# Parking x in eight pieces instead of one transfer, reloading it tile by tile, and loading p earlier, in one layer of a streaming encoder

## The reference

```
h = rmsnorm(x, g_mix_pre)
q_a, k_a, v_a, q_r, k_r, v_r, g_r, gate_a, gate_r = split_in(h @ w_in)
o_a = sliding-window attention with sinks (8 heads, 2 kv heads of 64)
o_r = retention (4 heads, key 128, value 256), group norm, * silu(g_r)
merged = sigmoid(gate_a) * (o_a @ w_branch_attn) + sigmoid(gate_r) * (o_r @ w_branch_ret)
x = x + rmsnorm(merged @ w_out, g_mix_post)
f = (silu(h @ w_ffn_gate) * (h @ w_ffn_up)) @ w_ffn_down      with h = rmsnorm(x, g_ffn_pre)
x = x + rmsnorm(f, g_ffn_post)
x = x + (p @ w_ple_proj) * sigmoid(x @ w_ple_gate)
```

## Time and profile before

| what | value |
|---|---|
| median of 3 runs | 1077.85 us (1077.6 to 1079.03) |
| span of the profiled execution | 1075.0 us (its own run time is not given) |
| TensorE, matmul busy | 1029.6 us, 96% |
| VectorE busy | 514.0 us, 48% |
| ScalarE busy | 333.8 us, 31% |
| GpSimd busy | 155.0 us, 14% |
| mean granted TensorE clock | 0.980 |
| DMA over the span | 88.63 MB, mean 82 GB/s |

### The profile page before, as it was taken

The page is one execution under the profiler, slowest core; times in us unless marked ns, Lnnn a source line. Parts: engine busy times, 40 slices in busy tenths (PEclk is TensorE's granted clock), DMA queues, the critical chain, the costliest instruction groups (busy, mean ns, idle before and its releaser), DMA issues.

```text
span 1075.0 us, 19829 instructions
## 1 busy us (share of the span) xinstructions
PE 1029.6 (96%) x7428; PEld 995.3 (93%) x7428; DVE 514.0 (48%) x855; ACT 333.8 (31%) x490; POOL 155.0 (14%) x162
## 2 busy tenths in 40 slices
PE   7999999999999999899949999999999999999697
PEld 5999899898999999899949999999999999999597
DVE  5554667666566433342295433432334444323842
ACT  5233434334434222123333322221222222222232
POOL 0221212121100000101272111100011111112500
PEclk9999999999999999999978999999999999999699
DMA  6722221221222232432211232223332322223032
GB/s 170 233 87 79 65 64 51 62 68 42 71 60 79 70 88 78 147 96 88 81 40 41 82 93 78 73 66 87 92 93 78 92 83 66 81 81 105 20 101 66
DMA packets 163818, 88.63 MB, mean 82 GB/s; under 512 B 14225, under 2 KB 162097, under 8 KB 163649
## 3 DMA queue, kind: packets, MB, share of 16 engines
q1 hardware_dynamic: 160256, 79.19, 25.6%
q0 software_dynamic: 1632, 7.23, 1.9%
q10 hardware_dynamic: 1888, 1.64, 0.5%
HBM read 82.08 MB, written 6.03 MB: 82 GB/s over the span
## 4 chain that ended last, share of the span: by engine, by line
PE 85%; DVE 5%; issue 3%; DMA 3%; ACT 1%; POOL 1%; POOLq 0%; DVEq 0%; SPq 0%; ACTq 0%
PE acc L467 77%; PE small L618 2%; DMA raw<-in_w_in 1%; PE small L633 1%; DMA raw<-in_w_branch_ret 1%; DVE wlo L1101 1%; DVE res L1417 1%; PE small L661 1%; PE small L665 1%; PE small L663 1%; ACT whi L790 1%; DVE yl L1428 1%; PE small L570 0%; ACT prob L850 0%; PE small L673 0%
## 5 line engine op out<-in xcount | busy, mean ns | idle before, releaser
L1101 DVE TENSOR_TENSOR wlo<-raw,whi 128x1024 fp32r<-128x1024 f32 (+3 forms) x156 | 181.1, 1161 | 337.4 <-ACT whi L790 337.0
L790 ACT ACTIVATE whi<-raw 128x1024 fp32r<-128x1024 f32 (+3 forms) x156 | 153.2, 982 | 436.9 <-PE acc L467 421.0
L467 PE MATMUL acc<-yh,whi 128*128 128x288 f32 x960 | 209.7, 299 | 25.3 <-DVE yl L1428 13.6
L467 PE MATMUL acc<-yh,wlo 128*128 128x288 f32 x960 | 208.2, 298 | 0.0
L467 PEld LDWEIGHTS acc<-yh,whi 128*128 128x128 f32 x960 | 156.2, 191 | 28.1 <-DVE yl L1428 14.9
L467 PE MATMUL acc<-yl,whi 128*128 128x288 f32 x832 | 179.5, 298 | 0.0
L467 PE MATMUL acc<-xh,whi 128*128 128x288 f32 x736 | 163.2, 303 | 2.1 <-DVE wlo L1101 2.0
L467 PE MATMUL acc<-xl,whi 128*128 128x288 f32 x736 | 157.4, 295 | 0.0
L467 PE MATMUL acc<-xh,wlo 128*128 128x288 f32 x736 | 156.8, 294 | 0.0
L467 PEld LDWEIGHTS acc<-yh,wlo 128*128 128x128 f32 x960 | 155.8, 191 | 0.0
L467 PEld LDWEIGHTS acc<-yl,whi 128*128 128x128 f32 x832 | 136.0, 192 | 0.0
(11 more groups left out here) (219 smaller groups left out, 1144.4 us busy)
## 6 DMA issues: line engine op xcount, KB each, us to landing
raw<-in_w_in SPq DMA_DIRECT2D x92, 256.0 KB, 3.1
raw<-in_w_ffn_gate SPq DMA_DIRECT2D x44, 256.0 KB, 3.1
raw<-in_w_ffn_up SPq DMA_DIRECT2D x44, 256.0 KB, 3.2
raw<-in_w_ffn_down SPq DMA_DIRECT2D x48, 192.0 KB, 2.4
raw<-in_w_branch_ret SPq DMA_DIRECT2D x16, 256.0 KB, 3.0
raw<-in_w_out SPq DMA_DIRECT2D x16, 256.0 KB, 2.9
raw<-in_w_ple_gate SPq DMA_DIRECT2D x16, 256.0 KB, 3.0
x_scratch<-x_t POOLq DMA_DIRECT2D x1, 2304.0 KB, 14.7
```

The lines of the kernel that those rows point to most:

```text
L467: ins = nc.tensor.matmul(acc[:, a, hf, 0:HALF], w[:, s, at:at + P], x(k)[:, hf * HALF:(hf + 1) * HALF], start=first and n == 0 and m == 0, ...
L790: nc.scalar.activation(whi[:, s, 0:n], raw[:, s, 0:n], ACT.Copy).then_inc(hi_ready, 1)
L1101: nc.vector.tensor_tensor(wlo[:, s, 0:n], raw[:, s, 0:n], whi[:, s, 0:n].bitcast(F32), ALU.subtract).then_inc(lo_ready, 1)
```

## The change

Four things change, nearly all in the stream of POOL:

- p and the caches are issued before `power(0)`, behind a new wait for the last quarter of x; the tables follow `power(0)`.
- x is parked by eight DMAs of one tile (288 KB) in place of one of 2304 KB. Two stand ahead of the first head, the others behind `head_job` of its six steps. They run in the first head alone (`isinstance(h, int)` is true only for the head that is written out).
- The reload of tile k waits for unit U_MRG2 + k instead of all eight for U_MRG2.
- Whoever waits for the park (ScalarE's first gate, POOL's reload) waits for all eight pieces.

```diff
@@ -937,7 +937,7 @@
                 if t == 0:
-                    act.wait_ge(x_saved, 16)
+                    act.wait_ge(x_saved, 16 * KD)
                 gate(w, a, sig[:, t // 2, t % 2, :])
@@ -1559,15 +1559,21 @@
             pool.dma_start(sink_row[:, :], sinks_in).then_inc(gains_in, 16)
-            power(0)
+            pool.wait_ge(x_in[QUARTERS - 1], 32)
             pool.dma_start(p_row[:, 0:RT - 1, :], p_p[0, 0].rearrange("(r p) n -> p r n", p=P)).then_inc(p_in, 16)
             pool.dma_start(p_row[0:DEC, RT - 1, :], p_s[0, 0]).then_inc(p_in, 16)
             pool.dma_start(ck_row[:, :], cache_k[0, 0].rearrange("n h d -> n (h d)")).then_inc(cache_in, 16)
             pool.dma_start(cva[:, :], cache_v[0, 0].rearrange("n h d -> n (h d)")).then_inc(cache_in, 16)
+            power(0)
             pool.dma_start(tab[:, T_ID + P:T_COLS], table_in[:, T_ID + P:T_COLS]).then_inc(tables_in, 16)
             pool.dma_start(rot[:, :, :], table_in[:, T_ROT:T_ALL].rearrange("p (a n) -> p a n", a=2)).then_inc(tables_in, 16)
-            pool.wait_ge(xt_copied, KD)
-            pool.dma_start(scratch, x_t[:, :, :].rearrange("p k n -> p (k n)")).then_inc(x_saved, 16)
+
+            def save_x(k):
+
+                if k == 0:
+                    pool.wait_ge(xt_copied, KD)
+                pool.dma_start(scratch[:, k * ROWS:(k + 1) * ROWS], x_t[:, k, :]).then_inc(x_saved, 16)
+
@@ -1632,6 +1638,8 @@
                     head_job(t, h, slot)
+                    if isinstance(h, int):
+                        save_x(t + 2)
                     pieces(2 * t + 1, r, rslot)
@@ -1644,15 +1652,17 @@
             pool.wait_ge(tables_in, 32)
+            save_x(0)
+            save_x(1)
             head(0, None, 0, None)
...
-            pool.wait_ge(unit_done, U_MRG2)
-            pool.wait_ge(x_saved, 16)
+            pool.wait_ge(x_saved, 16 * KD)
             for k in range(KD):
+                pool.wait_ge(unit_done, U_MRG2 + k)
                 pool.dma_start(res[:, k, :], scratch[:, k * ROWS:(k + 1) * ROWS]).then_inc(x_back, 16)
```

## The result

| | before | after |
|---|---|---|
| median of 4 runs | 1077.72 us (1077.05 to 1079.03) | 1070.98 us (1070.5 to 1071.94) |
| span of the profiled execution | 1075.0 us | 1068.7 us |
| mean granted clock | 0.980 | 0.983 |

The ratio is 0.9936 with a 95% interval of 0.9924 to 0.9948: the change takes 6.7 us (5.6 to 8.2) off. The direction was right, the gain was put too small by a quarter. Six more runs of the changed kernel later gave 1070.23 us, so the forecast missed by more than those 0.02 us. Where it comes from is mostly where the forecast looked for it, so the question is which terms were mis-sized.

What follows compares the result with a forecast made beforehand. TensorE, busy nearly throughout, was taken to bound the kernel, so time lay only in its stops and clock falls. Terms -0.53 and -4.50 took the span from 1075.0 to 1070.0; plus 2.85 gave 1072.8 us, range 1071.0 to 1075.3.

Steps and rivals of the forecast that it cites:

- Part 1: Start, POOL: p and caches ahead of power(0) wait for x and fall into an empty DMA stretch; cost 0.
- Part 4: First head: eight park issues on POOL, 0.55 us each, hide in its idle time; cost 0.
- the rival by the rule of the Trainium skill: First head: POOL's issues take some 3 us there, rotation comes 2.3 us late; 1075.1 us, chance 4%.
- Part 5: First head: each parked tile adds 1.0 us to a weight load (0.95 from one load), within spare time; cost 0.
- Part 6: Second merge: reloading x one tile per finished unit removes 3.07 us of stall and 1.43 of slow clock, -4.50 us.
- a fall in the clock without a stop: Second merge: the stall goes but 1.43 us of slow clock stay; 1074.3 us, chance 6%.
- late parks: First head: three parks hold a weight load, 3.3 us of stall and 1.43 of slow clock; 1077.5 us, chance 4%.
- a reload that still blocks: Second merge: a load keeps meeting reloads, the old stall stays, only 0.53 us goes; 1077.3 us, chance 3%.
- the first late load: Start, unit U_Q+2: load issued at 31.25 us, split only at 47.64, with 0.53 us of TensorE idle before the unit.
- The base: Whole run: the three-run median, 1077.85 us, lies 2.85 above the profiled span; that distance was kept for the forecast.
- part 3: Start: moving x's park away lets the U_Q+2 load land at about 38 us instead of 47.6; -0.53 us.

Runs made afterwards that it cites:

- experiments 2: The changed kernel with the reload of x put back into one burst at U_MRG2; 1076.28 us against 1076.91 for the kernel before, ratio 0.9993.
- 7: The changed kernel with SyncE holding the w_branch_ret load of the second merge pair until unit_done reaches U_MRG2 + 2; 1078.11 us.
- 8: The changed kernel with SyncE holding the w_branch_ret load of the second merge pair until unit_done reaches U_MRG2 + 3; 1082.12 us.
- the last set: Changed kernel again 1070.23 us; kernel before with per-unit reload alone 1071.54, plus p early 1071.33, plus late park 1070.65; kernel before 1077.22.

## Why the prediction came out low

**Right.** Both places, what bounds them, and the order of size. Part 1: p lands in the empty stretch, nothing is late behind it. Part 4: POOL's issues cost 0.55 us and hide; the rival by the rule of the Trainium skill (page "SBUF — State Buffer", "DVE blocks DMA") did not come, no issue in the head took longer than 0.58 us. (No row shows whether VectorE held the port during an issue, so this speaks for this kernel, not against the rule.) Part 5: no load of the first head landed later than 4.6 us after its issue (3.9 before). Its 0.95 us per tile mixed two measures, from issue to split for the slow load and from issue to landing for the fast one; by landing alone the slow load took 10.0 us, 0.9 per tile. Part 6: no ret load was late, and the slow clock went with the stall; experiments 2, 7 and 8 show that it belonged to the stall. In the first pair of profiles that term is all but exact: 4.50 forecast, 4.48 found. The rivals of a fall in the clock without a stop, of late parks and of a reload that still blocks did not come either.

**The terms that were mis-sized.** The places and waits were right; what failed is the sizing of the sum. Its base was 0.8 us too high, the first late load was priced at 0.53 us and measured 0.85, the merge at 4.50 from one light execution and measured 5.0 on average, and the rest at nothing and gave some 0.5.

1. *The base: the median "lies 2.85 us above the span, and I keep that distance".* No row stood behind that distance; it set the median of three runs against the span of another execution. An execution's own time lies 1.96 to 2.09 us above its span in the kernel before, as the later runs show, so the one profiled had run in about 1077.0. That is typical of the kernel, whose later medians are 1076.91 to 1077.22, while the three runs of the forecast happened to be slow. Worked from there, the same 5.0 us would have given 1072.0: of the 1.8 us between forecast and result, 0.8 are this base. It does not change the gain. And the distance is 1.77 to 1.84 us in the changed kernel: 0.2 us of the gain lie outside the span. With the park as one DMA it is 2.0 us, in pieces 1.8; why was not looked into.

2. *"-0.53 us" for the first late load (part 3).* Only the gap was priced. More than the gap went with it: the 120 matmuls behind it took 16.11 us before and 15.87 after; it is 16.1 in every profile with the gap and 15.87 to 15.94 in those without. The granted clock is 1.00 in both, and what slows them was not found. From x42 in the chain (22.90 us) to the first attention product, five profiles with before's start need 42.61 to 43.83 us, mean 43.18, and the changed kernel 42.34: 0.85 us. The gap itself was 0.53, 0.28, 0.30 and 1.03 us in four of the five and absent in the fifth, so the 0.53 was one draw of a term that scatters. The first profile's 1.15 has 0.17 in it that arose ahead of x42. The late park without p early stays at 42.54, so p early adds the last 0.2.

3. *"-3.07 - 1.43" for the merge (part 6).* Right for its execution, but that execution had the shortest stop of the six. The three profiles of the kernel before cost 5.0 us on average. That is half a microsecond more, the largest piece of the shortfall in the gain that is explained.

4. *Nothing for the rest.* What lies behind w_out, which the forecast left alone, gave 0.7 us in this pair, most of it in the slow stretches at 560 and 1010 us. Averaged over the three profiles of before and the two of the change it is 0.5. The stretches scatter (x102 takes 15.10 to 16.30 us), but not evenly: to x2976 the six profiles with a burst need 116.3 to 116.8 us and the ten without 115.6 to 116.4. The two held loads, which stop TensorE for longer, are among the ten at 116.31 and 116.23, so a stop in the merge alone does not do it. This stays open.

With 0.85, 5.0, 0.5 and 0.2 the terms make 6.55, against 6.7 measured with an interval of 5.6 to 8.2, and 7.0 in the second measurement. That the sum comes so near is in part luck, since every term scatters by some tenths. The range was too narrow because it took the spread of three runs, 1.4 us, where 29 runs spread over 5.2, and put no range on the stall itself, whose size came from one execution.

**Open.** Whether a changed start makes the burst heavier, or three profiles on either side fell so by chance. In time the pairs agree with the former (the reload is worth 4.8 to 5.4 us with before's start, 5.3 to 6.9 with the others, by the medians of the table), but a kernel's medians differ by 0.75 us when it is measured twice, and the two columns come from different sets; within the last set alone the reload is worth 5.7 us with before's start. There may also be executions with a cheap burst: the five fastest of the 29 runs of before (1074.05 to 1075.14 us) show a granted clock of 0.983, as most runs without a burst do, where the others show 0.978 to 0.981. None of those was profiled, so the 5.0 us average may leave out the light ones.

## What to carry to other kernels

A transfer that nobody waits for still holds up the small ones beside it. Look for the load that is due soonest, count the bytes that may be queued with it, and keep them under its spare time: here four tiles of 288 KB fitted and eight stopped TensorE. Look first for a place where no small load is due: there the park went as well in one piece as in eight. Pieces help only if they are also spread, as the reload shows, whose eight pieces in one burst did the harm. And a stall read from one profile has a range of its own; take two or three profiles before its size goes into a sum to a microsecond.

## What the runs showed of the hardware

- A stop of TensorE of 3.07 to 8.47 us is followed by a stretch at half clock that costs 1.3 to 2.5 us (eight profiles), with no clear relation to the length of the stop: 1.5 us behind 8.47, 2.5 behind 4.41. In some executions the engine begins at full clock, which falls within about a microsecond (first pair 0.53 us, kernel before); in others the clock fell during the stop and it begins at half (0.84 us). Stops of 0.28 to 1.03 us near 50 us left it at 1.00.
- A 256 KB load beside queued tiles of 288 KB landed 0.9 us later for each of four tiles (6.6 us), and took 10.0 to 11.9 us to land beside eight. DMA traffic with TensorE busy left the clock at 1.00 (241 GB/s).
- Executions of one unchanged kernel scatter by 5.2 us (29 of them), of which up to 2 us arise between TensorE's first product and x42, when x is transposed (9.4 to 11.5 us in the chains).
